# The two copies of TensorE's program behind the first experts meet in the second router instead of before the page attention

## The reference

```python
def mla_sample(q_lat, q_rope, rows_new, pool, page_table):      # layer 1, the page attention
    past = pool[page_table].reshape(Bd, -1, pool.shape[-1])
    allr = jnp.concatenate([past, rows_new], axis=1)
    ...
    return mla_attend(q_lat, q_rope, allr, mask)

def hier_moe(x, w_group, b_group, w_router, b_router, w_in, w_out):
    g_idx = jnp.argmax(t @ w_group + b_group, axis=-1)          # one of 4 groups
    e_logit = ...                                               # its 4 experts
    top_p, top_i = lax.top_k(jax.nn.softmax(e_logit, axis=-1), 2)
    ...
    h = jnp.einsum('td,edf->tef', t, w_in)
    a, b = jnp.split(h, 2, axis=-1)
    act = jax.nn.silu(a) * b * gates[..., None]
    return jnp.einsum('tef,efd->td', act, w_out)

for l in range(2):
    ...                                                         # attention of the layer
    x = layer_norm(ALPHA * x + mix, ln_g[l, 0], ln_b[l, 0])
    x = layer_norm(ALPHA * x + mem_attend(x, mk, mv, w_mem_q[l], w_mem_o[l]), ln_g[l, 1], ln_b[l, 1])
    x = layer_norm(ALPHA * x + hier_moe(x, ...), ln_g[l, 2], ln_b[l, 2])
```

## Time and profile before

| what | value |
|---|---|
| median of 3 runs | 1007.62 us |
| lowest, highest | 1007.56, 1010.48 us |
| the profiled execution's own time | 1007.25 us |
| its span (first to last instruction) | 1005.5 us |
| mean granted TensorE clock | 0.995 |

### The profile page before, as it was taken

The page is one execution under the profiler, slowest core; times in us unless marked ns, Lnnn a source line. Parts: engine busy times, 40 slices in busy tenths (PEclk is TensorE's granted clock), DMA queues, the critical chain, the costliest instruction groups (busy, mean ns, idle before and its releaser), DMA issues.

```text
span 1005.5 us, 18004 instructions
## 1 busy us (share of the span) xinstructions
PE 953.0 (95%) x7076; PEld 582.4 (58%) x7076; DVE 511.3 (51%) x1068; ACT 354.5 (35%) x891; POOL 254.7 (25%) x306
## 2 busy tenths in 40 slices
PE   7999999999999999899999999998999989999996
PEld 6887787878545856533333656557558674333332
DVE  0236630366838758532222385675578783323228
ACT  3335442021002445133333364565115442433323
POOL 3650000051600012445410014550000025552120
PEclk9999999999999999999999999999999999999999
DMA  9837100272203472889999722460266177999977
GB/s 319 205 85 252 49 1 3 82 207 88 74 1 54 161 287 107 307 336 411 417 414 414 294 97 53 94 193 14 69 206 272 43 249 234 359 416 416 417 218 182
DMA packets 76268, 203.62 MB, mean 203 GB/s; under 512 B 18104, under 2 KB 42464, under 8 KB 67088
## 3 DMA queue, kind: packets, MB, share of 16 engines
q1 hardware_dynamic: 59408, 153.31, 41.3%
q0 software_dynamic: 16768, 49.06, 15.7%
HBM read 184.46 MB, written 25.92 MB: 209 GB/s over the span
## 4 chain that ended last, share of the span: by engine, by line
PE 74%; DVE 12%; DMA 6%; ACT 6%; issue 2%; POOL 0%; SPq 0%; DVEq 0%; POOLq 0%; ACTq 0%
PE PS L1687 15%; PE PS L1468 10%; PE PS L1103 8%; PE PS L1704 7%; PE PS L1207 6%; PE PS L1499 3%; ACT arena L2133 2%; DMA ring<-in_moe_w_in_dram 2%; DMA arena<-in_moe_w_in_dram 2%; PE PS L1675 2%; PE PS L1126 2%; PE PS L1168 1%; PE PS L1825 1%; PE PS L1076 1%; ACT xT L2142 1%
## 5 line engine op out<-in xcount | busy, mean ns | idle before, releaser
L1687 PE MATMUL PS<-ring,arena 128*32 128x512 f32 x696 | 137.6, 592 | 3.5 <-DMA ring<-in_moe_w_in_dram 1.9
L2133 ACT ACTIVATE arena<-PS 32x520 f32<-32x520 f32 (+9 forms) x138 | 69.3, 515 | 160.9 <-PE PS L1103 39.0
L1687 PE MATMUL PS<-arena 128*32 128x512 f32 x600 | 106.8, 593 | 1.4 <-ACT arena L2427 1.4
L3217 DVE COPY arena<-PS 128x256 f32<-128x256 f32 x24 | 10.2, 425 | 176.5 <-PE PS L1695 176.5
L1103 PE MATMUL PS<-xT,ring 128*128 128x260 f32 x416 | 93.5, 385 | 3.5 <-DVE arena L2628 2.0
L1103 PEld LDWEIGHTS PS<-xT,ring 128*128 128x128 f32 x416 | 78.3, 190 | 17.6 <-DVE arena L2628 3.8
L2427 ACT ACTIVATE arena<-PS,lnc 128x128 f32<-128x128 f32 x184 | 66.9, 468 | 36.3 <-PE PS L1675 36.3
L1687 PEld LDWEIGHTS PS<-ring,arena 128*32 128x32 f32 x696 | 37.0, 110 | 58.1 <-issue 54.1
L1704 PE MATMUL PS<-ring,arena 128*32 128x512 f32 x408 | 65.4, 595 | 0.6 <-DVE arena L3217 0.6
L902 POOL DMA_INDIRECT y_tok<-arena,slot_dest x22 | 22.3, 1013 | 170.1 <-ACT arena L2465 155.6
L1207 PE MATMUL PS<-ring,xT 128*128 128x256 f32 (+2 forms) x336 | 65.2, 354 | 0.0
(11 more groups left out here) (450 smaller groups left out, 1818.1 us busy)
## 6 DMA issues: line engine op xcount, KB each, us to landing
ring<-in_moe_w_in_dram SPq DMA_DIRECT2D x29, 1024.0 KB, 11.9
arena<-in_moe_w_in_dram SPq DMA_DIRECT2D x25, 1024.0 KB, 10.9
ring<-in_moe_w_out_dram SPq DMA_DIRECT2D x17, 1024.0 KB, 11.8
ring<-in_w_in_even_dram SPq DMA_DIRECT2D x11, 1024.0 KB, 12.2
xT<-in_moe_w_in_dram SPq DMA_DIRECT2D x10, 1024.0 KB, 12.1
arena<-in_moe_w_out_dram SPq DMA_DIRECT2D x9, 1024.0 KB, 11.8
xT<-in_moe_w_out_dram SPq DMA_DIRECT2D x6, 1024.0 KB, 13.8
y_tok<-in_c_zeros_dram POOLq DMA_DIRECT2D x8, 512.0 KB, 10.7
```

The source lines that it names most:

```text
L1687: mm = pe.matmul(o[group(q), 0:512], xT_[:, k, group(q)], w(q, k), start=(k == 0), stop=(k == KD - 1), **quarter(q))
L2133: return act.activation(dst, src, ACT.Copy)
```

## The change

The ranks become a function of their own, `block_ranks(l)`, and leave `experts(l)`. For layer 0 the order is as before: `memory_stage(0)`, `block_ranks(0)`, `experts(0)`. For layer 1, `page_attention()`, `memory_stage(1)` and `block_ranks(1)` move into `behind_blocks()`, and so stand in both copies. The copies meet at the start of the new `experts(1)`, which begins with the tables. `n_rows` is a counter of the program that builds the kernel; it is set back so that the second copy waits for the same counts as the first.

```diff
+            routes = route.rearrange("p a n -> p (a n)")
+
+            def block_ranks(l):
                 key = ("rank", l)
                 o = open_(key)
-                routes = route.rearrange("p a n -> p (a n)")
                 pe.wait_ge(s["route_in"], 16)
...
                 close(pe.matmul(o[:, 512:512 + NT * NE], route[:, 1, :], new, start=True, stop=True), key)
+
+            def experts(l):
                 key = ("table", l)
                 o = open_(key)
...
                 latent_blocks()
                 first_page_scores()
+                counted = n_rows[0]
+                page_attention()
+                memory_stage(1)
+                block_ranks(1)
+                n_rows[0] = counted
...
             memory_stage(0)
+            block_ranks(0)
             experts(0)
-            page_attention()
-            memory_stage(1)
             experts(1)
```

More of the change, by code:

```diff
@@ L1628, in memory_stage @@
                     steps[key[0]](*key[1:])
-            def experts(l):
+            routes = route.rearrange("p a n -> p (a n)")
+            def block_ranks(l):
                 key = ("rank", l)
                 o = open_(key)
-                routes = route.rearrange("p a n -> p (a n)")
                 pe.wait_ge(s["route_in"], 16)
```

## The result

The changed kernel takes 1009.94 us (median of 20 runs, 1006.24 to 1015.44), the kernel before 1007.59 us (20 runs, 1003.49 to 1010.48). The ratio is 1.0028 with a 95% interval of 1.0015 to 1.0041: slower by some 2.8 us (the medians differ by 2.35), about what a measurement can tell from no change. The forecast was 1009.9 us, and the range 1005.8 to 1012.6 holds it. Both sides of the sum are in the trace, nearly at the size that the prediction gave them.

A forecast was written before the change was run, and what follows sets the result against it. TensorE, busy 953.0 of 1005.5 us, was taken to bound the kernel. A 5.4 us loss behind the ranks minus a 3.1 us gain in the page attention gave +2.3 on 1007.62: 1009.9 us, 8-in-10 range 1005.8 to 1012.6.

The forecast's parts named there:

- TensorE bounds the kernel, and a gain at 700 us lasts: From page attention to second router TensorE runs almost without a gap, so time gained at the start remains at the end.
- Term 1: Page attention: the jump between program copies leaves; second score row starts 1.33 us earlier, clock holds (1.75 us): 3.1 us gained.
- The jump is held by the wait for the counts: Second router's ranks: TensorE's jump begins only once the matmul waiting for VectorE's running counts starts, at about 821.5 us.
- rival B: Behind the ranks: the wait doesn't hold the jump, its fetch runs under the waits, loss near 0; 1004.6 us, chance 0.12.
- The jump's length under the loads: Behind the second router's ranks, with DMA engines full: 4.6 us quiet length plus 2.4 us surcharge, 7.0 us.
- Rival A: Behind the ranks: the jump is as quick as in the page attention, 4.6 us; time 1007.5 us, chance 0.22.
- rival C: Behind the ranks: the fetch waits until the loads are through, jump ends near 830.8, loss 8.6 us; 1013.1 us, chance 0.12.
- Products and clock: Behind the jump at the ranks: six unread matmul products take 2.6 us, and the fallen clock costs another 1.75 us.
- The loss at VectorE's read of the table: Second router, line 3130: read at 834.45 in place of 829.03, a loss of 5.4 us after 1.7 us are absorbed.
- The sum: Whole kernel: 5.4 us lost behind the ranks minus 3.1 us gained in the page attention, +2.3 us, giving 1009.9 us.
- Rival D: Both places: the jump isn't what the gap is, so nothing moves; 1007.6 us, chance 0.04.
- the branch's price: Opposing rule: a compare-and-branch takes about 108 ns, so the jump is worth 0.1 us anywhere and the net is nothing.

The follow-up runs named there:

- the second set of runs: The changed kernel measured once more with no edit, against the kernel before: 1008.73 us, ratio 1.0014 (0.9995 to 1.0034).
- the moved target of the earlier meeting: Kernel whose copies meet ahead of the ranks' waits, plus 16 unread products in the copy that doesn't run; against the kernel before: 1007.86 us, ratio 1.0014.

## Why the prediction was right

**TensorE bounds the kernel, and a gain at 700 us lasts.** Right: with nothing given back (the meeting in the page attention), the time fell by 3.2 to 4.5 us where the trace shows 3.0.

**Term 1, 3.1 us.** Measured 3.0. Both parts came: the gap ends on ScalarE's exponentials at 1.67 us, and the clock holds. All kernels that moved the meeting away show the same.

**The jump is held by the wait for the counts.** Right, against rival B. The standstill begins behind it, and it began ahead of it when the meeting was moved there. The Trainium skill (Perfetto Trace Analysis, Tensor Engine Instruction), by which the sequencer decodes on before an instruction's semaphores are satisfied, doesn't describe what these traces show of a jump (its block 6.9 us behind the unread products with the waits ahead of it, 4.3 without).

**The jump's length under the loads, 7.0 us.** It was 6.2 (825.63 − 819.46), so this term was too large by 0.8. It was made of 4.6 quiet and 2.4 for the traffic. The measured parts are 3.4 quiet at this place and 2.8 for the traffic: the first was overestimated, since the jump in the page attention, from which it came, is longer for a reason that stays open. The bounds of that length rested on a misreading as well: the block begins at 701.0, before TensorE's idle time (701.88 to 704.87) and not in it, and there was another at 700.0. The part for the traffic was nearly right, although its basis (40% of a load's delay) was a guess. Rival A (4.6 us) and rival C (a fetch that waits until the loads are through) both fall: the block came at 823.3 with the engines at 0.98 and 0.99.

**Products and clock.** The products took 4.6 us, and the prediction had 2.6 + 1.75 = 4.35. The first table came 6.46 us late (7.1 predicted), of which 1.6 were absorbed (1.7 predicted). The loss at VectorE's read of the table was 4.85 us (5.4).

**The sum.** 4.85 − 3.0 = +1.85 by the trace, with the gather's part on top. At the first matmul on the gathered rows the loss is 6.3 us in the first execution (19.00 against 12.7, of which 1.39 are the gather's) and 5.1 in the second (17.80), and net of the 3.0 it is 3.3 and 2.1. The medians differ by 2.35 us, and by 1.7 in the second set of runs. The forecast was +2.3. That it hit more closely than its terms is luck: they were too large by 0.1 and 0.55, and the gather's share was not in it.

**Rival D and the branch's price.** The Trainium skill (Advanced Engine Details and Errata, Control Flow Timing) gives some 108 ns for a compare-and-branch. A jump over a copy of some hundred lines cost 3.4 us with idle DMA engines and 6.1 us with busy ones here. The measurement decides: the figure doesn't hold where the target has to be fetched.

**What the prediction missed.** It treated the jump as a cost that goes with the program and asked only where it hurts less. The place where it costs nothing is five steps of the page attention behind the old one. And it didn't see that the loss could be had back by the order of products and jump (3.4 us measured).

## What to carry to other kernels

In this kernel a far jump of TensorE took 3.4 to 6.2 us, and the fallen clock behind it another 1.7 to 1.8, where its queue was short or a wait was open ahead of it. It cost nothing behind some 7 us of queued matmuls that wait for nothing. So, before such a meeting of paths is moved, look in the timeline for a row of long matmuls without idle time before it, and put it right behind that. Filler work, if it is needed, stands better ahead of a jump than behind it. And if an "issue" gap appears a few instructions behind a jump, see whether it goes when unused code ahead of the target is made longer.

## What the runs showed of the hardware

- The jump's length is mostly the time until its block of instructions begins to move: 1.0 us after the last wait with idle DMA engines, 3.8 us at a DMA share of 0.95 to 1.07. From there to the first matmul it is 2.3 us in both (823.3 to 825.63; 819.0 to 821.34), and up to 2.8 us in the other traces (820.05 to 822.87 with the moved target of the earlier meeting). The jump in the page attention of before is the exception, with 3.8 us. Under the loads the whole jump behind the ranks was 6.06 to 6.19 us in five traces.
- A second standstill behind the first came and went with code that is never executed. It was 3.96 us long in one kernel and 1.30 in another, where queued products covered part of it; from the start of its block to the next matmul it was 2.4 and 2.6 us. That the target lay a few instructions ahead of a block's end is inferred from both, and no view shows where a block ends.
- The clock held through 1.67 us of idle time and fell during or behind every standstill of 2.70 us or more (behind the 3.22 us: granted 0.79, then 0.50). In three executions (the kernel before, the one with the products first, and the one with the moved target of the earlier meeting) it also fell between 814 and 818 us, where TensorE had been busy for 1.98 of 2.00 us. Of the second:

```profile
814.00:816.00 2.00, 1.98 (x37) 1.84 (x36) 1.23 (x8) 0.31 (x2) 0.02 (x1) 0.78 1.03 377
816.00:818.00 2.00, 2.00 (x6) 1.49 (x5) 1.86 (x8) 0.00 (x0) 0.00 (x0) 0.50 1.01 229
```

  It cost next to nothing there, since the counts' matmul (818.65) started as soon as VectorE's counts were there (818.59). Why it fell stays open.
